# A hybrid decoder layer in fp32 halves: activations cross DRAM by features, and TensorE transposes none of them

## The reference, cut to what matters

```python
def decoder_layer(x, p, pool_buf, gla_state, conv_buf, start, ...):
    h = rmsnorm(x, g_pre_mix)
    z, q, k, v, glow, og = jnp.split(h @ w_in, SPLIT_IDX, axis=-1)
    gk = jax.nn.log_sigmoid((glow @ w_gk2 + b_gk2)) / GLA_GATE_NORMALIZER
    pool_out, pool_new = pool_mixer(z, pool_buf, start, w_pool, pool_scale)
    gla_out, gla_new = gla_mixer(q, k, v, gk, og, gla_state, gla_norm)
    mix = jnp.concatenate([pool_out, gla_out], axis=-1) @ w_o
    x = x + rmsnorm(mix, g_post_mix)
    f, conv_new = conv_ffn(rmsnorm(x, g_pre_ffn), conv_buf, w_up, w_conv, b_conv, w_down)
    x = x + rmsnorm(f, g_post_ffn)
    x = x + (p @ w_ple) * jax.nn.sigmoid(x @ w_ple_gate)
    return x, pool_new, gla_new, conv_new
```

## Time and profile before

| | |
|---|---|
| median of 3 runs | 2575.59 us (2574.25 to 2575.66) |
| profiled execution | 2575.31 us |
| its span, first to last instruction | 2573.6 us |
| PE / DVE / ACT / POOL busy, share of the span | 99% / 62% / 53% / 7% |
| mean granted TensorE clock | 0.998 |
| DMA | 409 MB, mean 159 GB/s |

### The profile page before, as it was taken

The page is one execution under the profiler, slowest core; times in us unless marked ns, Lnnn a source line. Parts: engine busy times, 40 slices in busy tenths (PEclk is TensorE's granted clock), DMA queues, the critical chain, the costliest instruction groups (busy, mean ns, idle before and its releaser), DMA issues.

```text
span 2573.6 us, 41685 instructions
## 1 busy us (share of the span) xinstructions
PE 2548.8 (99%) x16702; PEld 2493.6 (97%) x16702; DVE 1593.4 (62%) x2530; ACT 1353.8 (53%) x2157; POOL 172.5 (7%) x504
## 2 busy tenths in 40 slices
PE   9999999999999999999999999999999999999998
PEld 8999999999999999999999999999999999999998
DVE  6778755576655556665545566554556664657765
ACT  5455555564444456444445644444565444566554
POOL 3201000100000010000001000000100000000000
PEclk9999999999999999999999999999999999999999
DMA  8435456444434634444464444446444434656565
GB/s 250 131 124 192 144 152 214 138 162 146 152 121 126 222 132 159 152 148 125 120 219 140 164 148 151 124 121 213 144 164 147 147 120 127 203 178 201 186 182 170
DMA packets 121652, 409.15 MB, mean 159 GB/s; under 512 B 12814, under 2 KB 21686, under 8 KB 121462
## 3 DMA queue, kind: packets, MB, share of 16 engines
q1 hardware_dynamic: 121462, 406.51, 48.7%
HBM read 383.56 MB, written 22.89 MB: 158 GB/s over the span
## 4 chain that ended last, share of the span: by engine, by line
PE 95%; ACT 2%; DVE 1%; DMA 1%; issue 0%; SPq 0%; DVEq 0%; ACTq 0%
PE G L1698 29%; PE G L1700 29%; PE G L1699 29%; PE X L1757 2%; PE X L1691 1%; PE X L1694 1%; PE X L1825 1%; DMA w_lo<-kept_lo 1%; PE X L1831 0%; DMA stage<-in_w_up_units_dram 0%; PE G L1691 0%; PE X L1736 0%; ACT w_hi L746 0%; PE X L1810 0%; PE X L1743 0%
## 5 line engine op out<-in xcount | busy, mean ns | idle before, releaser
L1698 PE MATMUL G<-h_hi,w_hi 128*128 128x384 f32 (+2 forms) x3264 | 1061.6, 325 | 5.4 <-DVE w_lo L1195 2.3
L1700 PE MATMUL G<-h_lo,w_hi 128*128 128x384 f32 (+2 forms) x3264 | 1049.8, 322 | 0.0
L1699 PE MATMUL G<-h_hi,w_lo 128*128 128x384 f32 (+2 forms) x3264 | 1049.5, 322 | 0.0
L746 ACT ACTIVATE w_hi<-stage 128x1024 fp32r<-128x1024 f32 (+1 forms) x505 | 524.0, 1038 | 408.4 <-DMA stage<-in_w_up_units_dram 238.7
L1195 DVE TENSOR_TENSOR w_lo<-stage,w_hi 128x1024 fp32r<-128x1024 f32 (+1 forms) x505 | 604.2, 1196 | 170.8 <-ACT w_hi L746 170.2
L1698 PEld LDWEIGHTS G<-h_hi,w_hi 128*128 128x128 f32 x3264 | 615.2, 188 | 11.4 <-DVE w_lo L1195 3.1
L1699 PEld LDWEIGHTS G<-h_hi,w_lo 128*128 128x128 f32 x3264 | 615.5, 189 | 0.9
L1700 PEld LDWEIGHTS G<-h_lo,w_hi 128*128 128x128 f32 x3264 | 615.2, 188 | 0.0
L1698 PE MATMUL G<-y_hi,w_hi 128*128 128x384 f32 (+2 forms) x1056 | 346.3, 328 | 0.0
L1700 PE MATMUL G<-y_lo,w_hi 128*128 128x384 f32 (+2 forms) x1056 | 339.6, 322 | 0.0
L1699 PE MATMUL G<-y_hi,w_lo 128*128 128x384 f32 (+2 forms) x1056 | 339.5, 321 | 0.0
(11 more groups left out here) (239 smaller groups left out, 2654.6 us busy)
## 6 DMA issues: line engine op xcount, KB each, us to landing
stage<-in_w_up_units_dram SPq DMA_DIRECT2D x264, 512.0 KB, 3.5
w_lo<-kept_lo SPq DMA_DIRECT2D x107, 512.0 KB, 4.6
stage<-in_w_down_units_dram SPq DMA_DIRECT2D x96, 448.0 KB, 3.3
w_whole<-in_w_in_units_dram SPq DMA_DIRECT2D x72, 512.0 KB, 3.6
stage<-in_w_o_units_dram SPq DMA_DIRECT2D x48, 512.0 KB, 3.5
stage<-in_w_down_units_dram SPq DMA_DIRECT2D x48, 512.0 KB, 3.6
w_whole<-in_w_gate_units_dram SPq DMA_DIRECT2D x35, 512.0 KB, 3.7
stage<-in_w_in_units_dram SPq DMA_DIRECT2D x24, 512.0 KB, 4.4
```

What stands on the lines that cost most here:

```text
L746: act.activation(w_hi[s][:, 0:parts, :], whole[:, 0:parts, :], ACT.Copy).then_inc(hi_made, 1)
L1698: pe.matmul(ps[:, 0:w], l_hi, r_hi[:, 0:w], start=start, stop=False)
L1699: pe.matmul(ps[:, 0:w], l_lo, r_hi[:, 0:w], start=False, stop=False)
L1700: return pe.matmul(ps[:, 0:w], l_hi, r_lo[:, 0:w], start=False, stop=stop)
```

## The change

The host lays x and p out by tiles and features (`x_feat`, `p_feat`: for each tile, partition by block by token) and the states by features, and turns the outputs back. On the chip `turn_x`, `turn_p`, `turn_y` and all transposes of states go, 324 in all, with `copy_x`, `copy_y` and ScalarE's copies to `xr`. x is loaded straight into `xr`, p into `p_in`; `square_x` reads `xr`; `p_split` and `p_rest` take both blocks of p in one instruction each; `gate` adds into a new buffer `y_out`, which takes the place of `x_tok`/`y_tok` and shares it with `Z`, `p_in` and the gate's scratch, and waits once per tile for `z_saved` of the next tile. `evacuate_gate` waits for the sum of two blocks before rather than for its transpose.

```diff
+Y_PIECES = (((0, 3), (3, 6), (6, 8)), ((0, 4), (4, 7), (7, 8)))
...
             def load_x(t):
-                p0, np_, ns = TILES[t]
-                for c in range(chunks(t)):
-                    x_loaded.did(sp.dma_start(x_tok[:, c, :], x_prompt[0, p0 + P * c:p0 + P * c + P, :]), t, c)
...
+                x_loaded.did(sp.dma_start(xr[t % 2][:, :, 0:width(t)], of_tile(x_feat, t, KD)), t)
...
+            def store_y(t, a):
+                first, last = Y_PIECES[t == LAST][a]
+                sp.wait_ge(*y_added.at(t, last - 1))
+                y_stored.did(sp.dma_start(of_tile(y_feat, t, KD)[:, first:last, :], y_out[:, first:last, 0:width(t)]), t, a)
...
             def load_first_x():
...
+                for a in range(KD // 2):
+                    two = slice(2 * a, 2 * a + 2)
+                    sp.dma_start(xr[0][:, two, 0:width(0)], of_tile(x_feat, 0, KD)[:, two, :]).then_inc(first_x_loaded[a], 16)
...
+                if (kind, m) == ("up", 24) and 1 <= t < LAST:
+                    sp.wait_ge(*y_added.at(t - 1, KD - 1))
                     load_x(t + 1)
+                if (kind, m) == ("up", 40) and t == 0:
+                    sp.wait_ge(small_stored, 16 * 2)
+                    load_x(1)
...
-            def take_x(t, m):
-                act.wait_ge(*x_turned.at(t, m))
...
+            def square_x(t, m):
+                x = xr[t % 2][:, m, :]
                 if t:
+                    act.wait_ge(*x_loaded.at(t))
+                    square(x, sq_x, total_x, t, m, x_squared, x_added)
                 else:
-                    first_square(X[m % 4], sq_x, total_x, m, x_squared, first_x_taken)
+                    act.wait_ge(first_x_loaded[m // 2], 16)
+                    first_square(x, sq_x, total_x, m, x_squared, first_x_taken)
...
                 if m >= 2:
-                    act.wait_ge(*y_turned.at(t, m - 2))
+                    act.wait_ge(*y_added.at(t, m - 2))
...
                 dve.wait_ge(*gated.at(t, m))
-                y_added.did(dve.tensor_tensor(x, x, xr[t % 2][:, m, 0:w], ALU.add), t, m)
...
+                if m == 0:
+                    dve.wait_ge(*z_saved.at(min(t + 1, LAST)))
+                y_added.did(dve.tensor_tensor(y_out[:, m, 0:w], x, xr[t % 2][:, m, 0:w], ALU.add), t, m)
...
             for m in range(KD):
-                turn_x(0, m)
-                if m:
-                    first_sum(X[4], sq_x, total_x, m - 1, x_squared, first_x_taken)
-            first_sum(X[4], sq_x, total_x, KD - 1, x_squared, first_x_taken)
+                first_sum(X[4], sq_x, total_x, m, x_squared, first_x_taken)
```

355 lines of the change are left out of this document (89 added, 266 removed).

## The result

The changed kernel takes **2536.79 us** (median of 4 runs, 2535.13 to 2538.45) against 2575.62 (4 runs, 2574.25 to 2575.98): ratio 0.985, 95% interval 0.9833 to 0.9867, 38.8 us less. The profiled execution took 2537.6 us, its span is 2535.9 (before: 2575.3 and 2573.6).

A forecast was written before the change was run, and what follows sets the result against it. TensorE's queue, busy 99% of the span, was taken as the bound. Stream 32.5, start 2.0 and end 1.1 sum to 35.6 us off 2575.3, forecasting 2539.7 us, range 2533.5 to 2546 us held at 0.80.

The forecast's parts named there:

- The price of a transpose: In TensorE's queue: each transpose costs 0.112 us of matmul spacing, not its duration of 272 ns.
- The term of 30.5 us: In the stream: 272 of the 324 removed transposes at 0.112 us each gain 30.5 us.
- p behind `in` 1 of tile 1: Behind `in` 1 of tile 1: without six transposes for p the next matmul starts 1.1 us sooner.
- Tile 0's last gates: Ahead of tile 0's first `up` unit: VectorE is the bound, so removing nine transposes gains 0.
- The second and third rival: Second: VectorE takes gains back, 2550 us, chance 0.09 (over 2546); third: tile 0's gates run ahead, 2533.5 us, chance 0.06.
- Tile 1's last gates: Ahead of tile 1's first `up` unit: transposes and `sig` wait would bring 2.1 us, VectorE's low half caps it at 0.9.
- The start: Before the first product: unit 0's load lands earlier, at 9.6, root starts at 14.0; 2.0 us gained, ends 0.5 and 4.
- the lower end: At the start: only 0.5 us gained if TensorE, without transposes filling its waits, falls to its half clock.
- The end: After the last sum: transposes and copy go, the last sigmoid starts sooner; 1.1 us gained, ends 0.7 and 1.3.
- What costs nothing: Whole kernel: dropped copies, squares from SBUF, p's halves, DMAs, SP's order and the new VectorE wait change no time.
- the wait for `z_saved`: VectorE's new wait ahead of each tile's first sum: 35 us of air; as rival, late POOL gives 2590 us, chance 0.02.
- the duration as the price: Rival for all 324 transposes: each costs its 0.272 us, 88 us gained, 2487 us; chance 0.01.

The follow-up runs named there:

- spare_at_gates: Changed kernel plus twelve unread transposes in tile 0's last gates (23.72 us, 23.70 without) and twelve in tile 1's `up` (185.13 us, 183.80 without).
- spare_x: Changed kernel plus 112 transposes with unread results in `down` of tiles 0 to 4, where x was transposed; 2551.85 us.
- before_again: Kernel before the change, unaltered, executed again for a second trace; 2577.23 us, one run.
- sums_on_gpsimd: Changed kernel with the sums of gate and activation of tiles 0 to 4 on GpSimd, not VectorE; tile 0's last gates 23.36 us, 0.34 less.
- before: Kernel before the change, its first profiled execution; 2575.3 us.

## Why the prediction was right, point by point

- **The price of a transpose** (0.112 us from three of them in rows 4): 0.111 in `spare_at_gates`, 0.114 in `spare_x`, 0.114 by the table's `down` of tiles 1 to 3 (2.74 / 24). The term of 30.5 us was up to 2% too small by that, some 0.5 us.
- **p behind `in` 1 of tile 1** (1.1): `in` of tile 1 gained 1.2, the same stretch of tiles 2 to 4 the 0.7 of six steps. Right in size. The six transposes themselves were the dearer ones in tile 1: they and the next product start 1.08 us after the pack's beginning, in tile 2 of the same trace 0.58 (the row below, and 854.53). Why they stand further apart there no run tells.

```profile
853.95 0.82 PE L1691 MATMUL X<-ident,p_tok 128*128 128x128 f32 x6
```

- **Tile 0's last gates** (0): 0.01 us. Right, and for the reason given: 0.02 for a pack of twelve, 0.9 for one pair of VectorE's instructions less. Of its side remarks one held, the unit starts 0.05 us behind its low half; the other was too low, TensorE idles there for 5.1 us and not 2 to 4, since the waits ahead of gates in the same stretch grew too. The prediction's reading of the clock in rows 8 was off as well: 0.07 x 23.9 = 1.7 us is the time that the half clock costs, the stretch at half clock is twice as long. The second and third rival need the cost, so their sums stand.
- **Tile 1's last gates** (0.9): 0.93 once the late load is set apart, 1.2 against `before_again`, 2.2 against the execution that I had read. The number is right by luck, the step behind it failed: 2.1 us were to be gained, and VectorE's low half, at 1016.98, was to cap them at 0.9. But that low half was 1.65 us late by a load, and so was the wait for `sig` of 1.1 us that made up half of the 2.1. Without the load nine transposes are all there is to gain, and VectorE caps nothing: 1.26 us of air in tiles 2 and 3 became 0.33, in tile 1 as well, where the prediction had the unit start within 0.2 us of its low half. The same trace told it, since the low halves of tiles 2 and 3 stand 1.65 us earlier in their stretches. How near the cap is, `spare_x` shows: there a late load moved tile 3's low half by 0.9 us, the unit started 0.05 us behind it, and the stretch took 21.42 us instead of 20.80.
- **The start** (2.0, ends 0.5 to 4): 2.77 in the profiled pair. The mis-sized step is the landing of unit 0: issued 1.17 us earlier (2.82 for 3.99, forecast 1.1) and 6.0 us on its way, where I had kept 6.7; it landed at 8.8, not 9.6. From there on the sum nearly held: root at 12.91, 4.1 behind the landing, forecast 4.4. What the lower end stood for happened too: TensorE fell to its half clock between the squares in four of nine executions. But it cost less than the end allowed, the first product then stands at 16.7 to 17.0, which is 1.6 to 1.9 us gained and not 0.5; that this lies nearest to the forecast of 16.5 is chance, since the forecast had no half clock in it.
- **The end** (1.1): 1.2.
- **What costs nothing**: ScalarE's and VectorE's copies, p's halves, the squares, SP's new order and the wait for `z_saved` show in no wait of TensorE and in no stretch, the last `ple` left open. Right.
- **The sum**: 35.6 forecast, 37.7 measured in the profiled pair: the stream 33.7 for 32.5, the start 2.8 for 2.0, the end 1.2 for 1.1. The stream's 1.2 us are 0.5 of step price, 0.1 for p, and 0.5 that is left of larger pieces of both signs which belong to single executions: 1.3 in tile 1's gates and 1.3 in the last tile's `up` of the one trace, less 2.1 at the last `ple` of the other. So it is luck in part that the total came this near; in the two later pairs the medians differ by 35.6 us, the forecast's own number, and by 38.1.
- **The rivals**: the duration as the price is refuted by `spare_x`. The time taken back by VectorE in tiles 2 to 4 didn't happen (20.80 us in each, no wait, but 0.33 us of air is left); it happened only where it already was. The granted clock did not fall further over the whole run (mean 0.999 for 0.998), but in four executions it did at the start. More gained through tile 0's gates did not happen, although the half clock went there. The wait for `z_saved` showed nothing.

## What to carry to other kernels

Price an instruction of a full queue by what it does to the starts of its neighbours, not by its duration; a pack of spare copies in a place of full load measures it to a hundredth of a microsecond. Cut the timeline into stretches at fixed points of the program and run both kernels twice, before a difference in one of them is given a cause: most stretches repeated to 0.02 us here, four varied by 1 to 5, and those looked like effects. Before you take another engine's end as a cap, compare it with the same place in the other tiles: here it was 1.65 us late for a load, and the cap and half of what it was to cap came from that.

## What was not expected of the hardware

- A VectorE instruction of 0.61 us took 1.23 beside a GpSimd sum of 1.78 us (`sums_on_gpsimd`), so that three sums moved to GpSimd brought 0.34 us and not 1.6.
- At the start the granted clock from 9 to 15 us is 1.00 in all three executions with transposes between the squares and 0.72 to 0.80 in four of nine without.
- The same 512 KB load landed after 4.4 or 7.4 us in two executions of one kernel, and the same 25 us of one program ran at a granted clock of 0.93 or 0.79 (`before`, `before_again`).
